# First layer of a two-layer hybrid encoder: attention heads placed between projection units, output projection by weight rows, one-pass gate sums, the norm taken bank by bank

## The chip, the cores and the metric

The kernel runs on one core of a Trainium2 chip. The metric is the device time of one launch in microseconds (us). The changed kernel is compared with the kernel before on the same inputs.

## The reference

One sequence of 256 tokens, width 1024, passes two layers. Each layer has a mixer and a channel mixer, each with an RMS norm ahead of it and a residual addition behind it.

```python
# layer 0, mixer A
h = rmsnorm(x, mix_norm_g[0]); m = rmsnorm(mem, mem_norm_g[0])
mk, mv = split(m @ w_mem_kv[0])                       # 4 heads of 64, 256 memory tokens
q, k, v, fl, qm = split(h @ w_in_a[0])                # 12 FoX heads of 64; fl: 12 gate columns
cum = cumsum(log_sigmoid(fl + b_forget))              # along the sequence
s = (q @ k.T) * 64**-0.5 + cum[query] - cum[key]      # causal, in blocks of 128 queries
y_self = softmax(s) @ v
y_mem = softmax((qm @ mk.T) * 64**-0.5) @ mv
x = x + concat(y_self, y_mem) @ w_out[0]
x = x + swiglu(rmsnorm(x, ffn_norm_g[0]))             # dense, inner width 2816
# shared K and V are projected from x; layer 1: differential attention (6 heads) beside
# memory attention, then 8 experts of inner width 3584, top 2 of 8; a final norm
```

## The kernel before, in words

Weights arrive in units of 128 x 2048 f32 (1 MB) through a ring of 6 `raw` slots that SP fills. ScalarE (ACT) casts a unit to `whi` (L521), VectorE (DVE) subtracts to get `wlo` (L809); both are rings of 3 slots. The activations are split in the same way into `op_hi` and `op_lo`. A product of two f32 matrices is then three one-pass matmuls in the rounded type, hi·hi, hi·lo and lo·hi (`product`, L1359 to L1361). A projection unit p of `PROJ` is 256 weight columns: 8 blocks of the contraction, 3 passes and 2 halves, 48 matmuls of 256 columns (`project`). It fills one PSUM bank, and DVE moves it out (`take(p)`, L851).

Each engine executes its own list in order, and semaphores bind the lists. TensorE's list for layer 0 is:

- `norm_transposes(0)` and unit 0, `norm_transposes(1)` and unit 1: mk and mv from the memory tokens.
- Units 2 to 11: q0 to q2, k0 to k2, v0 to v2, qm. Between them stand the transposes of norm 2 (the memory norm of layer 1), the gate columns (`small_product`), their transposes and the cumulated sums (L1520, L1521).
- `attention_pe(0)`: 12 FoX heads, then 4 memory heads. Scores run up to 4 heads ahead of the values. The score of a FoX head (L1430, L1435, L1438) has, for each of the two query tiles, an f32 matmul of q and k over 64 rows (128 or 256 keys), an f32 matmul over 12 rows that adds -cum[key] (`ident[0:12, h]` by `ncum`), and a bf16 one that adds the causal mask. Three 128x128 transposes of the probabilities (L1456; four for a memory head) and the values (L1483, L1485, L1488) follow. Between them DVE takes maxima (L985, L986) and scales the probabilities (L1026 to L1029); ACT takes exponentials (L605, L607) and copies transposed probabilities (L634).
- Units 12 to 15: the output projection, each 256 columns of `w_out` over all 8 blocks, added to X by `take`. Unit 16 (mk of layer 1), the transposes of norm 3 (`norm_transposes(3)`), unit 17, and then the dense channel mixer.

In the lists of ACT and DVE the splits of coming units stand between these steps. DVE does `angles` (rotary angles, a chain of small operations, L925 to L949) beside late q/k/v units, while nobody waits for them until layer 1.

A norm is: squares with row sums on ACT (L538 or L529), mean and epsilon on DVE (L821), the square root on ACT (L541), reciprocal (L824) and scaling by row and gain (L837, 4 pieces of 128x512) on DVE, then 16 transposes on TensorE (L1372), `op_hi` on ACT (L550) and `op_lo` on DVE (L846). For norm 4, behind the channel mixer of layer 0, DVE waits for the last matmul of the last down-projection unit, adds four banks to X (L1108), ACT squares them, and one mean and one root serve both token tiles:

```python
            split_lo(U_KV + 1)
            dve.wait_ge(unit_used, U_KV)
            # four additions bank -> X, then
            norm_dve(4, X, 5, parts=2)
            norm_fill_lo(4)
```

## Time and profile before

| | |
|---|---|
| Time, three runs | 1620.61, 1621.83 (median), 1622.0 us |
| Span of the profiled execution, from first to last instruction | 1619.5 us (2.3 us under the median) |
| TensorE matmuls busy | 1542.1 us, 95% |
| DVE, ACT busy | 73%, 59% |
| TensorE's share of the chain that ended last | 94% |
| Mean granted TensorE clock | 0.944 of full speed |

"Granted clock" is the share of TensorE's full 2.4 GHz that the chip let through; it has two levels here, 1.00 and 0.50. The busy time of matmuls is modelled and overlapping, so the distance from one start to the next says more than a duration. A row "x2" for one f32 matmul means that it is recorded as two. A stretch "A:B" is in microseconds from the start of the span.

### The profile page before, as it was taken

The page shows a single profiled execution, that of the slowest core. Times are in us where ns is not written, and L with a number is a line of the kernel's source. Part 1 is how long each engine was busy: PE and PEld are TensorE (multiplying, and loading weights), DVE is VectorE, ACT ScalarE, POOL GpSimd, SP SyncE. Part 2 cuts the span into 40 slices and gives each one's busy share as a digit, 9 for nine tenths or more (in the row PEclk, how much of TensorE's full clock was granted, in tenths as well). Part 3 has the DMA queues.
Part 4 walks back from the last instruction along what each step waited for, and adds up shares of the span by engine and source line. Part 5 has one row for each costly group of instructions (what it writes and reads, how often), then busy time and mean ns, then how long its engine had stood idle before and what let it go on. Part 6 is the DMA issues. An engine that isn't in the chain of part 4 may idle for free.

```text
span 1619.5 us, 21334 instructions
## 1 busy us (share of the span) xinstructions
PE 1542.1 (95%) x8083; PEld 1291.0 (80%) x8083; DVE 1181.3 (73%) x1013; ACT 954.4 (59%) x885; POOL 14.4 (1%) x44
## 2 busy tenths in 40 slices
PE   4999999999899879999999999999999999999996
PEld 4975598999796668887887887887888888888884
DVE  4642254445675657988989889888888988888885
ACT  4432344343433537777776767767776776776774
POOL 2000000000000000000000000000000000000000
PEclk8985599999897879999999999999999999999998
DMA  9640044645542237999999998998998998998991
GB/s 301 199 156 0 1 144 156 208 156 201 185 145 94 110 138 271 380 338 334 372 357 332 372 378 307 372 376 312 370 374 311 370 374 311 369 383 284 324 352 76
DMA packets 210235, 428.93 MB, mean 265 GB/s; under 512 B 6800, under 2 KB 62096, under 8 KB 210176
## 3 DMA queue, kind: packets, MB, share of 16 engines
q1 hardware_dynamic: 208880, 424.18, 73.4%
q0 software_dynamic: 1296, 3.96, 1.0%
q8 instruction: 38, 0.62, 0.2%
q14 instruction: 21, 0.17, 0.0%
HBM read 427.06 MB, written 1.05 MB: 264 GB/s over the span
## 4 chain that ended last, share of the span: by engine, by line
PE 94%; DVE 3%; DMA 1%; ACT 1%; issue 1%; DVEq 0%; SPq 0%; ACTq 0%
PE bank L1359 27%; PE bank L1361 27%; PE bank L1360 27%; PE bank L1430 3%; PE bank L1634 2%; PE bank L1709 2%; PE bank L1635 1%; PE bank L1435 1%; DMA raw<-in_w_mem_kv_dram 1%; PE bank L1483 1%; PE bank L1456 1%; PE bank L1372 1%; PE bank L1438 1%; PE bank L1425 1%; DVE wlo L809 0%
## 5 line engine op out<-in xcount | busy, mean ns | idle before, releaser
L809 DVE TENSOR_TENSOR wlo<-raw,whi 128x2048 fp32r<-128x2048 f32 x397 | 907.4, 2290 | 216.4 <-ACT whi L521 215.3
L521 ACT CAST whi<-raw 128x2048 fp32r<-128x2048 f32 x397 | 758.1, 1914 | 276.7 <-PE bank L1361 263.6
L1359 PE MATMUL bank<-whi,op_hi 128*128 128x512 f32 (+1 forms) x1248 | 456.7, 366 | 5.4 <-DVE op_lo L1169 1.7
L1361 PE MATMUL bank<-whi,op_lo 128*128 128x512 f32 (+1 forms) x1248 | 450.6, 361 | 0.0
L1360 PE MATMUL bank<-wlo,op_hi 128*128 128x512 f32 (+1 forms) x1248 | 450.3, 361 | 0.0
L1359 PEld LDWEIGHTS bank<-whi,op_hi 128*128 128x128 f32 x1248 | 237.2, 190 | 44.1 <-DVE wlo L809 3.4
L1361 PEld LDWEIGHTS bank<-whi,op_lo 128*128 128x128 f32 x1248 | 237.1, 190 | 36.1
L1360 PEld LDWEIGHTS bank<-wlo,op_hi 128*128 128x128 f32 x1248 | 237.4, 190 | 33.7
L1359 PE MATMUL bank<-whi,h2T_hi 128*128 128x512 f32 x536 | 210.8, 393 | 0.0
L1361 PE MATMUL bank<-whi,h2T_lo 128*128 128x512 f32 x536 | 208.9, 390 | 0.0
L1360 PE MATMUL bank<-wlo,h2T_hi 128*128 128x512 f32 x536 | 208.7, 389 | 0.0
L1359 PE MATMUL bank<-op_hi,whi 128*128 128x256 f32 x512 | 146.1, 285 | 16.7 <-DVE op_lo L846 13.7
L1360 PE MATMUL bank<-op_lo,whi 128*128 128x256 f32 x512 | 145.5, 284 | 0.0
L1361 PE MATMUL bank<-op_hi,wlo 128*128 128x256 f32 x512 | 145.5, 284 | 0.0
L1361 PEld LDWEIGHTS bank<-whi,h2T_lo 128*128 128x128 f32 x536 | 100.6, 188 | 21.4
L1360 PEld LDWEIGHTS bank<-wlo,h2T_hi 128*128 128x128 f32 x536 | 100.8, 188 | 20.0
L1359 PEld LDWEIGHTS bank<-whi,h2T_hi 128*128 128x128 f32 x536 | 100.7, 188 | 19.9
L1359 PEld LDWEIGHTS bank<-op_hi,whi 128*128 128x128 f32 x512 | 99.0, 193 | 17.7 <-DVE op_lo L846 14.1
L1360 PEld LDWEIGHTS bank<-op_lo,whi 128*128 128x128 f32 x512 | 99.0, 193 | 0.4
L1361 PEld LDWEIGHTS bank<-op_hi,wlo 128*128 128x128 f32 x512 | 98.9, 193 | 0.0
L738 ACT CAST h2T_hi<-bank 128x512 fp32r<-128x512 f32 x56 | 32.9, 588 | 66.3 <-PE bank L1709 66.3
L985 DVE TENSOR_REDUCE negm<-bank 128x1 f32<-128x128 f32 (+1 forms) x32 | 10.3, 323 | 66.3 <-PE bank L1438 58.2
(247 smaller groups left out, 1034.8 us busy)
## 6 DMA issues: line engine op xcount, KB each, us to landing
raw<-in_w_gate_up_moe_dram SPq DMA_DIRECT2D x223, 1024.0 KB, 6.8
raw<-in_w_down_moe_dram SPq DMA_DIRECT2D x109, 1024.0 KB, 6.9
raw<-in_w_gate_up_dense_dram SPq DMA_DIRECT2D x22, 1024.0 KB, 5.1
raw<-in_w_down_dense_dram SPq DMA_DIRECT2D x11, 1024.0 KB, 5.0
raw<-in_w_in_a_dram SPq DMA_DIRECT2D x10, 1024.0 KB, 11.6
raw<-in_w_out_dram SPq DMA_DIRECT2D x8, 1024.0 KB, 5.1
raw<-in_w_kv_shared_dram SPq DMA_DIRECT2D x6, 1024.0 KB, 5.1
raw<-in_w_mem_kv_dram SPq DMA_DIRECT2D x4, 1024.0 KB, 11.8
```

Source lines behind the costliest of these rows:

```text
L521: a.copy(whi[:, c % SPLIT, :], src).then_inc(hi_ready, 1)
L738: a.copy(h2T_hi[j % 2][:], bank[tb_bank(f"T{j}")][:]).then_inc(h2_hi, 1)
L809: d.tensor_tensor(wlo[:, c % SPLIT, :], src, whi[:, c % SPLIT, :].bitcast(F32), ALU.subtract).then_inc(lo_ready, 1)
L1359: m.matmul(dst, sh, mh, start=start and i == 0, stop=False)
L1360: m.matmul(dst, sh, ml, start=False, stop=False)
L1361: last = m.matmul(dst, sl, mh, start=False, stop=stop and i == n - 1)
L1372: last = m.transpose(bank[g][:, P * c:P * (c + 1)], hn[:, t, P * k:P * (k + 1)], ident[:])
L1425: mm = m.matmul(b[:, MEM * t:MEM * (t + 1)], qmT[po:po + HD, c, sl], mkT[layer][po:po + HD, c, :], start=True, stop=True)
L1430: m.matmul(b[:, o0:o0 + w], qT[po:po + HD, c, sl], kT[po:po + HD, c, 0:w], start=True, stop=False)
L1435: m.matmul(b[:, o0:o0 + w], ident[0:FOX_H, h:h + 1].to_broadcast([FOX_H, P]), ncum[:, 0:w], start=False, stop=False)
L1634: m.matmul(dst, st_hi, mv_hi, start=start, stop=False)
L1709: last = m.transpose(bank[tb_bank(f"T{j}")][:, P * c:P * (c + 1)], h2[j % 2][:, P * c:P * (c + 1)], ident[:])
```

## The change

- The heads of layer 0 are handled one by one in `HEADS0`, 4 memory heads first and then 12 FoX heads, and TensorE's list becomes a loop of 17 steps. Step s issues the dense work of `DENSE0[s]` (a whole unit or one half of it, 12 units in all), then transposes of head s, values of head s-1, and scores of head s+2. The lists of ACT and DVE are loops over the same steps.
- Unit order: mk, mv, qm, then q, k, v for four heads at a time.
- Output projection by weight rows (`out_rows`): a unit is 256 rows of `w_out`, all 1024 columns, summed over the four units in banks 4 to 7. It is 24 matmuls of 512 columns. The last unit stays behind the loop, after `norm_transposes(2)`, which moves there from the second unit.
- The term -cum[key] is stored as a rounded part in rows 0 to 11 and the remainder in rows 32 to 43 of `ncum`, zero elsewhere, and enters by one pass over 128 rows with a 0/1 column of `pick`, in place of the f32 matmul.
- DVE and ACT do the rotary angles before the attention; `take(1)`, the split of unit 4 and `take(P_QM)` follow them on DVE.
- Norms 3 and 4 are taken bank by bank: each bank of the last product raises a semaphore, and the first token tile is normalised ahead of the second (`sum_norm`). The split of unit U_KV+1 now stands behind the norm on DVE. Other norms have mean, root and reciprocal for each tile apart.
- The gain of norm 2 shares the tile of the first gain and is loaded by GpSimd after norm 0 has been applied.

```diff
-PROJ = ([("mk", 0), ("mv", 0)]
-        + [("q", i) for i in range(3)] + [("k", i) for i in range(3)] + [("v", i) for i in range(3)] + [("qm", 0)]
-        + [("out", i) for i in range(4)] + [("mk", 1), ("mv", 1)]
+PROJ = ([("mk", 0), ("mv", 0), ("qm", 0)]
+        + [(what, i) for i in range(3) for what in "qkv"]
+        + [("rows", i) for i in (3, 0, 1, 2)] + [("mk", 1), ("mv", 1)]
...
+HEADS0 = [("mem", h) for h in range(MEM_H)] + [("fox", h) for h in range(FOX_H)]
+N0 = len(HEADS0)
+DENSE0 = [[(3, 0), (3, 1)], [(4, 0), (4, 1)], [(5, 0), (5, 1)], [(6, 0), (6, 1)], [(7, 0), (7, 1)], [(8, 0)], [(8, 1)],
+          [(9, 0), (9, 1)], [(10, 0)], [(10, 1)], [(11, 0)], [(11, 1)], [(12, 0)], [(12, 1)], [(13, 0), (13, 1)],
+          [(14, 0)], [(14, 1)]]
+def ended_in(s):
+    return [p for p, c in DENSE0[s] if c == 1]
+def takes(p):
+    return sum(what != "rows" for what, _ in PROJ[:p + 1])
...
+def proj_bank(p):
+    if p < P_OUT0:
+        return 4 + p % 3
+    return 4 + (p - P_M1 if p < P_KV else p % 4)
...
+        pick = sb("pick", [P, FOX_H], F32R)
         negm = sb("negm", [P, 32, NT])
...
+            pool.dma_start(start_gain[2], mem_norm_g[1:2, :].to_broadcast([P, D])).then_inc(start_gain_in[2], 16)
             for n in range(3, 8):
                 load_gain(n)
...
-            split_until(4)
+            norm_squares(2, tok, mem_in)
+            for t in range(NT):
+                norm_sqrt(2, t)
             act.wait_ge(small_in, 16 * 9)
             a.copy(small_hi[:], small_w[:]).then_inc(small_hi_ready, 1)
+            split_until(4)
+            act.wait_ge(ang_ready, 1)
+            a.activation(sinv[:], ang[:, 1], ACT.Sin)
+            a.activation(cosv[:], ang[:, 2], ACT.Sin).then_inc(sin_ready, 1)
...
+                if s >= 3:
+                    act.wait_ge(pT_ready, s - 2)
+                pr, b = prob[s % 3], bank[s % 2]
+                a.activation(pr[:, 0:w0], b[:, 0:w0], ACT.Exp, bias=negm[:, s, 0:1], accum_out=rsum[:, s, 0:1])
+                a.activation(pr[:, w0:w0 + w1], b[:, w0:w0 + w1], ACT.Exp, bias=negm[:, s, 1:2],
+                             accum_out=rsum[:, s, 1:2]).then_inc(exp_done, 1)
...
+            exp0(0)
+            exp0(1)
+            split_until(6)
...
+            for s in range(N0 + 1):
+                for u in ended_in(s):
+                    split_until(u + 4)
+                if s < N0:
+                    copy0(s)
+                if s and s % 2 == 0:
+                    pair_hi0(s // 2 - 1)
+                if s + 2 < N0:
+                    exp0(s + 2)
+            norm_fill_hi(2)
+            sqrt_table()
+            sum_norm(3, x_out, 0)
...
+            def sum_norm(n, banks, ready, counts, done):
+                for q in range(4):
+                    if q == 3:
+                        norm_mean(n, 0, 2)
+                    t, cols = q // 2, slice(512 * (q % 2), 512 * (q % 2 + 1))
+                    dve.wait_ge(ready[q], counts[q])
+                    d.tensor_tensor(X[:, t, cols], X[:, t, cols], bank[banks + q][:], ALU.add).then_inc(done, 1)
+                norm_scale(n, 0)
+                apply_gain(n, X, n, 0, 0)
+                norm_mean(n, 1, 2)
+                apply_gain(n, X, n, 0, 1)
+                norm_scale(n, 1)
+                for h in range(2):
+                    apply_gain(n, X, n, 1, h)
...
+            dve.wait_ge(ident_ready, 1)
+            d.tensor_tensor(pick[:], ident[:, 0:FOX_H], ident[:, 32:32 + FOX_H], ALU.add).then_inc(pick_ready, 1)
+            angles_start()
+            angles(1)
+            angles(2)
+            take(1)
+            split_until(5)
+            lambda_dots()
+            take(P_QM)
+            dve.wait_ge(flT_ready, 1)
+            d.tensor_copy(small_T, bank[7][0:FOX_H, 0:SEQ]).then_inc(flT_out, 1)
...
+                cum = bank[7][0:FOX_H, SEQ:2 * SEQ]
+                step(d.tensor_scalar(ncum[0:FOX_H, :], cum, -1.0, None, ALU.mult))
+                d.scalar_tensor_tensor(out=ncum[32:32 + FOX_H, :], in0=cum, scalar=-1.0,
+                                       in1=ncum[0:FOX_H, :].bitcast(F32), op0=ALU.mult,
+                                       op1=ALU.subtract).then_inc(ncum_ready, 1)
...
+            max0(0)
+            max0(1)
+            forget_sums()
+            split_until(6)
+            normalise0(0)
+            for s in range(N0 + 1):
+                for u in ended_in(s):
+                    if PROJ[u][0] != "rows":
+                        take(u)
+                if s == 0:
...
+                if s == 1:
+                    decay_rows()
+                if s + 2 < N0:
+                    max0(s + 2)
+                if s + 1 < N0:
+                    normalise0(s + 1)
+                if s and s % 2 == 0:
+                    pair_lo0(s // 2 - 1)
+                for u in ended_in(s):
+                    split_until(u + 4)
+            norm_fill_lo(2)
+            sum_norm(3, 4, [acc_ready] * 3 + [unit_used], [1, 2, 3, P_M1], x_out)
...
             split_lo(U_KV)
+            sum_norm(4, 0, [acc_ready] * 3 + [unit_used], [4, 5, 6, U_KV], x_added)
             split_lo(U_KV + 1)
-            dve.wait_ge(unit_used, U_KV)
-            for t in range(NT):
-                for h in range(2):
-                    cols = slice(512 * h, 512 * (h + 1))
-                    d.tensor_tensor(X[:, t, cols], X[:, t, cols], bank[2 * t + h][:], ALU.add).then_inc(x_added, 1)
-            dve.wait_ge(x_added, 4)
-            norm_dve(4, X, 5, parts=2)
...
+            def out_rows(p, parts=(0, 1)):
+                _, i = PROJ[p]
+                first, final = p == P_OUT0, p == P_M1 - 1
+                hi, lo = op_hi[Y_BUF[0]], op_lo[Y_BUF[0]]
+                if 0 in parts:
+                    pe.wait_ge(lo_ready, p + 1)
+                    pe.wait_ge(fill_lo, int(FILL[1]) + 2 * (p - P_OUT0) + 2)
+                    if first:
...
+                for t in parts:
+                    sl = slice(P * t, P * (t + 1))
+                    for h in range(2):
+                        cols = slice(512 * h, 512 * (h + 1))
+                        last = product(bank[4 + 2 * t + h][:],
+                                       [((hi[:, 2 * i + k, sl], lo[:, 2 * i + k, sl]), (wh[:, k, cols], wl[:, k, cols]))
+                                        for k in range(2)], start=first, stop=final)
+                        if final and not (t == 1 and h == 1):
+                            last.then_inc(acc_ready, 1)
+                if 1 in parts:
+                    last.then_inc(unit_used, 1)
...
+            def score0(s):
+                kind, h = HEADS0[s]
+                if s >= 2:
+                    pe.wait_ge(exp_done, s - 1)
+                if s == 0:
+                    pe.wait_ge(proj_out, takes(P_QM))
+                if kind == "fox" and h == 0:
+                    pe.wait_ge(ncum_ready, 1)
+                    pe.wait_ge(pick_ready, 1)
+                if kind == "fox" and h % 4 == 0:
+                    pe.wait_ge(proj_out, takes(P_A + 3 * (h // 4) + 1))
...
+                    w, o0 = P * (t + 1), P * t
+                    m.matmul(b[:, o0:o0 + w], qT[po:po + HD, c, sl], kT[po:po + HD, c, 0:w], start=True, stop=False)
+                    m.matmul(b[:, o0:o0 + w], pick[:, h:h + 1].to_broadcast([P, P]), ncum[:, 0:w], start=False,
+                             stop=False)
+                    mm = m.matmul(b[:, o0 + w - P:o0 + w], ident_bf[:], causal[:], start=False, stop=True)
...
+                pe.wait_ge(pT_out, s + 1)
+                if kind == "fox" and h % 4 == 0:
+                    pe.wait_ge(proj_out, takes(P_A + 3 * (h // 4) + 2))
+                if s % 2 == 0 and pr:
+                    pe.wait_ge(fill_lo, int(FILL[1]) + pr)
...
-            for p in range(P_A, P_OUT0):
-                project(p)
-                if p == P_A:
...
-                    pe.wait_ge(logf_ready, 1)
-                    pe.wait_ge(consts, 1)
-                    m.matmul(bank[3][0:FOX_H, 256:512], fg[:, 2, 0, :], upper[:], start=True, stop=False)
-                    m.matmul(bank[3][0:FOX_H, 384:512], fg[:, 2, 1, :], upper[:, 0:P], start=False,
-                             stop=True).then_inc(cum_ready, 1)
-            pe.wait_ge(ncum_ready, 1)
-            pe.wait_ge(proj_out, P_OUT0)
-            attention_pe(0)
-            for p in range(P_OUT0, P_M1 + 1):
-                project(p)
+            project(P_QM)
+            pe.wait_ge(small_lo_ready, 1)
+            pe.wait_ge(small_hi_ready, 1)
+            small_product(bank[7], 1, 0, FOX_H).then_inc(flT_ready, 1)
+            score0(0)
+            score0(1)
+            pe.wait_ge(flT_out, 1)
+            small_transposes(bank[7], FOX_H).then_inc(fl_ready, 1)
+            for s in range(N0 + 1):
+                for p, c in DENSE0[s]:
+                    if PROJ[p][0] == "rows":
+                        out_rows(p, (c,))
+                    else:
+                        project(p, (c,))
+                if s == 1:
+                    forget_cum()
+                if s < N0:
+                    transposes0(s)
+                if s:
+                    values0(s - 1)
+                if s + 2 < N0:
+                    score0(s + 2)
+            norm_transposes(2)
+            out_rows(P_M1 - 1)
+            project(P_M1)
             norm_transposes(3)
             project(P_M1 + 1)
```

## Rows read from the trace of the kernel before

**Rows 1.** The page's costliest groups of instructions: busy us, mean ns, idle before.

```profile
L809 DVE TENSOR_TENSOR wlo<-raw,whi 128x2048 fp32r<-128x2048 f32 x397 | 907.4, 2290 | 216.4 <-ACT whi L521 215.3
L521 ACT CAST whi<-raw 128x2048 fp32r<-128x2048 f32 x397 | 758.1, 1914 | 276.7 <-PE bank L1361 263.6
```

**Rows 2.** Busy time by stretch: us, PE, PEld, DVE, ACT, POOL, clock, DMA, GB/s.

```profile
106.90:199.65 92.75, 90.45 (x253) 48.96 (x253) 26.28 (x89) 28.00 (x91) 0.00 (x0) 0.54 0.06 20
109.50:121.50 12.00, 12.00 (x29) 6.23 (x29) 2.90 (x7) 2.85 (x13) 0.00 (x0) 0.50 0.26 87
```

**Rows 3.** Timeline, TensorE, first FoX scores: start, us, instruction.

```profile
106.90 0.46 PE L1430 MATMUL bank<-attn 64*128 64x128 f32 x2 [1.18 <-DVE attn L868]
107.29 0.48 PE L1435 MATMUL bank<-ncum,ident 12*128 12x128 f32 x2
107.70 0.23 PE L1438 MATMUL bank<-causal,ident_bf 128*128 128x128 bf16 x1
...
108.49 0.69 PE L1435 MATMUL bank<-ncum,ident 12*128 12x256 f32 x2
109.11 0.23 PE L1438 MATMUL bank<-causal,ident_bf 128*128 128x128 bf16 x1
109.27 0.79 PE L1430 MATMUL bank<-attn 64*128 64x128 f32 x2
```

**Rows 4.** Timeline, TensorE, one FoX head in the middle of the attention.

```profile
155.49 0.79 PE L1430 MATMUL bank<-attn 64*128 64x128 f32 x2
...
159.53 0.85 PE L1456 MATMUL bank<-ident,prob 128*128 128x128 f32 x3
160.31 1.11 PE L1483 MATMUL bank<-probT,attn 128*64 128x256 f32 x2
...
161.78 0.79 PE L1430 MATMUL bank<-attn 64*128 64x128 f32 x2
```

**Rows 5.** Timeline, TensorE, memory heads of layer 0, then one of layer 1.

```profile
194.72 0.66 PE L1456 MATMUL bank<-ident,prob 128*128 128x128 f32 x4
195.31 0.65 PE L1483 MATMUL bank<-probT,mv 128*64 128x256 f32 x2
...
196.32 0.65 PE L1456 MATMUL bank<-ident,prob 128*128 128x128 f32 x4
...
540.43 1.14 PE L1425 MATMUL bank<-attn 64*128 64x256 f32 x8
```

**Rows 6.** Timeline, TensorE, behind unit 2: transposes, unit 3, gate columns.

```profile
47.87 1.91 PE L1372 MATMUL bank<-ident,hn 128*128 128x128 f32 x16
49.54 0.36 PE L1359 MATMUL bank<-op_hi,whi 128*128 128x256 f32 x1
...
55.36 0.28 PE L1359 MATMUL bank<-op_hi,small_hi 128*12 128x256 f32 x1
```

**Rows 7.** Timeline, DVE, scaling of norm 2.

```profile
40.06 2.74 DVE L837 SCALAR_TENSOR_TENSOR hn<-tok,stat,attn 128x512 f32<-128x512 f32 x4
```

**Rows 8.** Busy time by stretch: from the first to the last operation of `angles`.

```profile
98.44:99.85 1.41, 1.41 (x14) 1.41 (x13) 1.21 (x8) 0.00 (x0) 0.00 (x0) 1.00 0.10 22
104.53:106.16 1.63, 1.19 (x10) 0.98 (x9) 1.39 (x10) 0.00 (x0) 0.00 (x0) 1.00 0.16 38
```

**Rows 9.** Busy time by stretch: norm 4, and memory attention of layer 1.

```profile
426.50:430.00 3.50, 0.00 (x0) 0.00 (x0) 2.54 (x6) 2.56 (x8) 0.00 (x0) 1.00 0.84 283
430.50:440.00 9.50, 7.25 (x33) 6.88 (x34) 7.92 (x10) 4.15 (x5) 0.53 (x1) 0.50 0.18 57
542.00:555.00 13.00, 8.70 (x50) 5.58 (x50) 9.50 (x33) 9.49 (x30) 0.00 (x0) 1.00 0.00 0
```

**Rows 10.** Timeline, DVE and TensorE, norm 4.

```profile
426.23 2.48 DVE L1108 TENSOR_TENSOR X<-X,bank 128x512 f32<-128x512 f32 x4 [1.15 <-PE bank L1361]
...
430.45 2.74 DVE L837 SCALAR_TENSOR_TENSOR hn<-X,stat,gain 128x512 f32<-128x512 f32 x4
...
436.39 0.58 PE L1359 MATMUL bank<-whi,op_hi 128*128 128x256 f32 x1 [1.40 <-DVE op_lo L846]
```

More of the change, by code:

```diff
@@ L331, in proj_source @@
             if what == "out":
-                return out_v[p >= P_OUT1][:, :, c:c + WIDE]
+                return out_v[1][:, :, c:c + WIDE]
+            if what == "rows":
+                return out_v[0][:, 2 * i:2 * i + 2, :]
             if what == "kd":
@@ L625, in fill @@
                     act.wait_ge(pv_ready, rb0 + r + 1)
-                    a.copy(op_hi[Y_BUF[layer]][:, c, :], bank[5 + (r // 2) % 2][:, 0:SEQ]).then_inc(fill_hi, 1)
+                    a.copy(op_hi[Y_BUF[1]][:, c, :], bank[5 + (r // 2) % 2][:, 0:SEQ]).then_inc(fill_hi, 1)
                 exps(AHEAD - 1)
@@ L702, in _ @@
             out_squares(P_OUT1, [U_KV + 13, U_MOE, U_MOE + 1])
-            norm_act(6, None, None)
+            for t in range(NT):
+                norm_sqrt(6, t)
             norm_fill_hi(6)
@@ L974, in attention_dve @@
-            def attention_dve(layer):
-                scores, outs, last = attention_plan(layer)
-                sb0, rb0 = S_BASE[layer], R_BASE[layer]
+            dve.wait_ge(ident_ready, 1)
[8 more added lines that the diff above has]
+            dve.wait_ge(flT_ready, 1)
@@ L977, in attention_dve @@
+            norm_fill_lo(2)
+            sum_norm(3, 4, [acc_ready] * 3 + [unit_used], [1, 2, 3, P_M1], x_out)
+            split_lo(U_FFN)
+            take(P_M1)
+            norm_fill_lo(3)
+            split_lo(U_FFN + 1)
+            take(P_M1 + 1)
+            def attention_dve():
+                scores, outs, last = attention_plan()
+                sb0, rb0 = S1, R1
                 done = [0]
@@ L1408, in small_transposes @@
                 return last
-            def attention_pe(layer):
-                scores, outs, last_s = attention_plan(layer)
-                sb0, rb0 = S_BASE[layer], R_BASE[layer]
+            def score0(s):
+                kind, h = HEADS0[s]
+                if s >= 2:
+                    pe.wait_ge(exp_done, s - 1)
[6 more added lines that the diff above has]
+                    pe.wait_ge(proj_out, takes(P_A + 3 * (h // 4) + 1))
+                b = bank[s % 2]
+                po, c = HD * (h % 2), h // 2
+                for t in range(NT):
+                    sl = slice(P * t, P * (t + 1))
+                    if kind == "mem":
+                        mm = m.matmul(b[:, MEM * t:MEM * (t + 1)], qmT[po:po + HD, c, sl], mkT[0][po:po + HD, c, :],
+                                      start=True, stop=True)
+                        continue
+                    w, o0 = P * (t + 1), P * t
[3 more added lines that the diff above has]
+                    mm = m.matmul(b[:, o0 + w - P:o0 + w], ident_bf[:], causal[:], start=False, stop=True)
+                mm.then_inc(score_ready, 1)
@@ L1498, in attention_pe, with forget_cum @@
                 values(len(outs) - 1)
+            def forget_cum():
+                pe.wait_ge(logf_ready, 1)
+                pe.wait_ge(consts, 1)
+                b = bank[7]
+                m.matmul(b[0:FOX_H, SEQ:2 * SEQ], fg[:, 2, 0, :], upper[:], start=True, stop=False)
+                m.matmul(b[0:FOX_H, SEQ + P:2 * SEQ], fg[:, 2, 1, :], upper[:, 0:P], start=False,
+                         stop=True).then_inc(cum_ready, 1)
             pe.wait_ge(ident_ready, 1)
@@ L1560, in ffn_down @@
                                         for k, s in enumerate(sls)], start=first, stop=final)
+                        if final and not (t == 1 and h == 1):
+                            last.then_inc(acc_ready, 1)
                 last.then_inc(unit_used, 1)
```

389 lines of the change are left out of this document (210 added, 179 removed).

## The prediction

> **What bounds the kernel now.** I read the page's shares first: TensorE is busy 95% of the span and has 94% of the chain that ended last, so the time is TensorE's list, its idle gaps and its clock. The costliest groups say that the splits of weights, the largest work of DVE and ACT, cost 2.29 and 1.91 us a unit [rows 1]; a projection unit costs TensorE 5.8 us [rows 6], so in the projections both engines have room. Then I read busy time by stretch. The attention of layer 0 lasts 92.75 us, with TensorE busy 90.45 of them at a mean clock of 0.54, DVE and ACT busy 26 and 28, and almost no transfer; inside it stands a stretch of 12 us, busy throughout, at 0.50 [rows 2]. The reader is to see a stage in which the bounding engine never rests and yet runs at 1.2 GHz.
>
> **Prices at either clock.** The first FoX score is still at the full clock: 106.90 to 109.27, 2.37 us, of which the two gate matmuls take 0.41 and 0.62 [rows 3]. In the middle a head takes 6.29 us at half clock: score 4.04, three transposes 0.78, values 1.47 [rows 4]. The score is the only part seen at both, a factor of 1.70. A memory head at the full clock has 0.59 for transposes and 1.01 for values, and its score 1.14 [rows 5].
>
> **The change part by part.** The sum is made against the span of 1619.5 us; the median of the runs shown is 2.3 us more, and I add the difference at the end.
>
> *Dense work.* Units 2 to 17 stay sixteen units of 5.8 us [rows 6]; the row-wise output units have half as many matmuls of twice the columns, the same stream. The transposes of norms 2 and 3 (1.67 us each [rows 6]), the gate columns and the cumulated sums only move. Zero, if the clock stays full in them.
>
> *Gate sums.* Two f32 matmuls of 1.03 us together [rows 3] become two one-pass matmuls over the same columns. The nearest row is the projection, 5.82 us for 48 passes of 256 columns, 0.12 each [rows 6]. I take 0.23 for both. The bounds are no gain (a stationary operand with stride 0 is in no row for this type) and all of 1.03, 0 to 12.4 us over 12 heads; I take the value nearest to the projection's row. The split of ncum adds one DVE operation, once.
>
> *Heads at the full clock.* This is the main term. FoX: score 2.37 - 1.03 + 0.23 = 1.57, transposes three quarters of 0.59 = 0.44, values 1.47 by 1.70 = 0.86; 2.87 us, 34.4 for twelve. Memory: 1.14 + 0.59 + 1.01 = 2.74, 11.0 for four. Together 45.4 us, where 92.75 and the 1.18 of idle ahead of them [rows 2, 3] stood: 93.9.
>
> Whether the clock stays full is read from where it fell. It was 1.00 on the first FoX score and 0.50 from 109.5 on [rows 2, 3], and 1.00 through 3.5 us of idle behind the channel mixer, then 0.50 [rows 9]. In the memory attention of layer 1 it stayed 1.00 for 13 us though TensorE was busy only 8.70 of them, with no projection at all [rows 9]. So short gaps do not lower it; a stretch of nothing but FoX scores and heads did. In the new loop a head's 2.87 us stand between pieces of 2.9 or 5.8 us of projection. I take full clock throughout the loop.
>
> The Trainium skill, page "TensorE: Matmul & The Clock Gate", section "Why this matters for your kernels", asks for no idle gaps of TensorE above about 3 us between bursts of matmuls. By this rule alone a list that is never idle should not lose its clock, and the main term of this sum would be nothing; the 12 busy microseconds at 0.50 contradict it [rows 2], and the measurement decides. For a real idle gap, as in norm 4 [rows 9], the trace agrees.
>
> *A new wait ahead of the loop.* `score0(0)` needs `take(P_QM)`. On DVE, behind the scaling of norm 2, which ends at 42.8 [rows 7], there stand in order: small_lo (0.3, estimate), the split of unit 3 (2.3), pick and the start of the angles (0.8, estimate), two passes of angles (1.41 and 1.63 [rows 8]), `take(1)` (0.6). That is 49.8. (Small terms without a row, here and below, are estimates on the scale of rows 7 and 8: 0.69 for a piece of 128x512, 0.2 for an operation on a few columns, and down from there.) ACT may cast unit 4 only after the two sines, which wait for the angles: 49.5 + 0.4 + 1.9 = 51.8. Then DVE has the split 2.3, the lambda sums 0.7 and `take(P_QM)` 0.7: 55.5. TensorE has finished unit 2 at 47.87 [rows 6] and the gate columns 2.8 later, at 50.7, and waits 4.8 us. Queued behind the waiting instruction is everything of the loop. Bounds: 3 us if the small operations overlap, 6.5 if the waits between them add up. The gap costs clock too: as in norm 4 I expect the fall, two memory scores at half (2.28 by 1.70, 1.6 more), and the first dense piece at half for about as long as behind norm 4, where the product resumed at 436.39 and the clock was still 0.50 up to 440.0 [rows 9, 10]: near 4 us at half speed, 2.0 lost. Together 8.4; bounds 3 and 12.
>
> *Other waits in the loop.* Probabilities of head s+1 are needed behind the dense piece of step s+1. DVE begins its maxima when that piece begins and needs 0.7 for them and 0.85 for the scaling, less than the shortest piece of 2.9 [rows 6]. The split behind it ends about 4.8 + 2.3 us past the end of unit u and is needed two units later. ACT needs 1.9 for the cast, then 0.5, 0.4 and 1.1. A take of 0.7 stands ahead of the maxima only where a unit ended, and lies beside 2.9 us of transposes, values and score. So zero; bounds 0 and 1 us a step. At the loop's end `norm_transposes(2)` waits with its fourth bank for the last pair, whose copy stands on ACT behind a cast: values 0.9, transposes 1.3, against 1.95 + 0.4 + 0.5 and a signal: 0.8 us of idle. The norm of layer 0's output then lies beside unit 16, as before.
>
> *Norm 4.* Before, the chain from the first addition to the product ran from 426.23 to 436.39 [rows 10]. Now three additions and three squares lie beside the last product. From 426.2: last addition 0.7, square 0.85, first reciprocal and piece beside it; mean and roots 0.7 net, remaining pieces to 430.5. Then the split of unit U_KV+1, 2.3, which used to lie beside the product and now stands ahead of the low halves; these take 2.5. Product at 435.4, a gain of 1.0. Without that split it would be 3. Bounds 0 and 3 (the latter with the clock kept). Norms 0 to 2 and 6 get a few operations of 0.17 more; where they lie on the path (norm 6) the first tile starts earlier: zero, bounds ±0.5.
>
> *The start.* One gain load of 0.5 MB goes behind norm 0 on GpSimd's queue. It competes with the first weights a little later and not less. Zero, bounds ±1.5. It is needed near 40 us and has over 20 us.
>
> **The sum.** 93.9 - 45.4 - 8.4 - 0.8 + 1.0 = 40.3 us. The span becomes 1579.2 and the median 1581.5 us.
>
> **The rivals.**
>
> *The clock falls in some steps.* Ten of the 17 steps hold only half a unit, so there 2.87 us of head stand by 2.9 us of dense work. For it: the fall on FoX scores with TensorE busy [rows 2, 3]. Against it: 13 us of thin memory attention at 1.00 [rows 9]. A step at half costs 5.8 by 0.70, 4.0 us. With half of the ten steps it is 20 us: 1602; with all ten 1622.
>
> *Hand-offs cost.* The signals of three engines cross in every step, and one late link (a take ahead of the maxima, a cast ahead of the copy) stops TensorE. At 0.7 us in 17 steps it is 12 us: 1593. Against it are the margins above, more than 1.3 us at each link.
>
> *Slower.* The mixture holds TensorE at half clock for the whole loop, so the dense work, full before, pays as well. Place: steps 0 to 16; price: 69 us of dense and 43 of heads by 0.70, 78 us, less the 40 gained: 1660. It decides from the point where the clock is at half for more than half of the loop. For it speaks only that the attention never recovered by itself in 85 us; against it that 4 us of projection brought it back each time.
>
> *The one pass is not what it says.* Where the one-pass gate matmul costs as much as the old pair, the heads come to 55 us: 1591.
>
> **Chances.** Forecast 0.72; some steps at half 0.10; hand-offs 0.08; one pass without gain 0.05; slower 0.05. The range reaches from 1572 (short wait, clock kept in norm 4, small products cheap) to 1602. About 0.2% is what a measurement of this kernel can tell from no change, 3.2 us; only the slower rival and the worst end of the clock's case are there. Faster 0.93, same 0.02, slower 0.05.
>
> **What would show it.** In the stretches of the changed profile, 60 to 175 us has a clock of 1.00 and TensorE busy over 95%. The gate line has two one-pass matmuls a head with starts 0.1 to 0.13 us before the next. One idle gap of 3 to 6.5 us stands ahead of the first memory score, released by DVE, and the clock is 0.50 behind it. Unit 17 ends near 197 us. The product behind norm 4 resumes about 9.3 us after the last matmul of the channel mixer. From there on every distance is as before. The forecast is wrong if clock rows of 0.50 recur past 65 us, if idle time ahead of the transposes or values adds up to more than 5 us, or if the later stages change by more than 2 us.

## The result and the profile after

The changed kernel takes **1577.42 us** (median of 4 runs, 1575.57 to 1578.95), beside 1621.22 us for the kernel before in the same session: a ratio of 0.9735, 95% interval [0.9722, 0.9748], 43.8 us less. The profiled execution of the changed kernel spans 1573.8 us, where the one before spanned 1619.5. Two executions of the kernels below, one of dense_first (2386.29 us) and one of turns_of_2 (2170.47 us), ran at mean granted clocks of 0.59 and 0.645 in place of some 0.95, and no ratio below uses them.

First the shares and the chain on the page after, then the two groups that answer to [rows 1].

```profile
PE 1495.9 (95%) x7963; PEld 1264.8 (80%) x7963; DVE 1181.2 (75%) x1030; ACT 953.9 (61%) x883; POOL 15.6 (1%) x45
...
PE 92%; DVE 4%; ACT 2%; DMA 1%; issue 1%; DVEq 0%; SPq 0%; ACTq 0%
...
L897 DVE TENSOR_TENSOR wlo<-raw,whi 128x2048 fp32r<-128x2048 f32 x397 | 907.4, 2290 | 202.2 <-ACT whi L556 201.2
L556 ACT CAST whi<-raw 128x2048 fp32r<-128x2048 f32 x397 | 758.1, 1914 | 271.3 <-PE bank L1516 257.7
```

TensorE still bounds the kernel at the same 95%, and DVE and ACT do the same work on weights in the same time. What went is TensorE's own time: 46.2 us less busy. Where, is seen in the busy time by stretch of the kernel after (columns as in [rows 2]): the wait ahead of the first score, the piece behind it, the whole loop, and the pieces behind the two later gaps.

```profile
50.15:53.93 3.78, 0.01 (x2) 0.00 (x1) 3.57 (x6) 1.63 (x3) 0.00 (x0) 1.00 0.09 18
53.93:57.50 3.57, 3.57 (x16) 2.74 (x17) 1.83 (x7) 0.78 (x3) 0.00 (x0) 0.52 0.94 291
57.50:170.90 113.40, 112.60 (x724) 92.08 (x723) 55.75 (x112) 49.53 (x102) 0.34 (x1) 1.00 0.34 109
206.86:211.10 4.24, 4.24 (x23) 4.24 (x24) 2.75 (x2) 0.20 (x1) 0.00 (x0) 0.60 0.72 225
392.50:395.50 3.00, 2.97 (x14) 2.97 (x15) 3.00 (x3) 0.00 (x0) 0.00 (x0) 0.52 0.74 258
```

The reader is to see the third row beside the first of [rows 2]: 0.54 has become 1.00, for 113 us. ("Dense" work is that of the projection units, matmuls of all 128 rows one behind the other.) All the idle time in those 113 us is one wait of 0.80. The timeline of TensorE shows it, and one head in the middle of the loop, between one dense piece, whose last matmul starts at 104.29, and the next, which starts at 107.26. It answers to [rows 3, 4, 6].

```profile
53.93 1.98 PE L1614 MATMUL bank<-mkT,attn 64*128 64x256 f32 x8 [3.77 <-DVE attn L988]
...
63.55 0.66 PE L1632 MATMUL bank<-ident,prob 128*128 128x128 f32 x4 [0.80 <-DVE prob L1100]
64.14 1.13 PE L1614 MATMUL bank<-mkT,attn 64*128 64x256 f32 x4
...
104.41 0.49 PE L1632 MATMUL bank<-ident,prob 128*128 128x128 f32 x3
104.83 0.65 PE L1648 MATMUL bank<-probT,attn 128*64 128x256 f32 x2
105.32 0.38 PE L1650 MATMUL bank<-probT,attn 128*64 128x128 f32 x2
105.63 0.48 PE L1618 MATMUL bank<-attn 64*128 64x128 f32 x2
106.04 0.33 PE L1619 MATMUL bank<-ncum,pick 128*128 128x128 f32 x1
106.21 0.23 PE L1621 MATMUL bank<-causal,ident_bf 128*128 128x128 bf16 x1
106.37 0.70 PE L1618 MATMUL bank<-attn 64*128 64x256 f32 x2
107.00 0.38 PE L1619 MATMUL bank<-ncum,pick 128*128 128x256 f32 x1
107.22 0.23 PE L1621 MATMUL bank<-causal,ident_bf 128*128 128x128 bf16 x1
107.26 0.36 PE L1514 MATMUL bank<-whi,op_hi 128*128 128x256 f32 x1
...
172.98 0.66 PE L1529 MATMUL bank<-ident,hn 128*128 128x128 f32 x4 [0.52 <-DVE op_lo L1107]
```

A FoX head takes 2.85 us in place of 6.29 [rows 4]: transposes 0.42, values 0.80, score 1.63. The two gate matmuls take 0.17 and 0.22 by the distance to the next start.

**One ruler for all kernels.** TensorE's first product starts at 27.19 us before and 26.52 after, and between 23.96 and 27.72 in the twelve kernels below, whose starts hardly differ. So I measure from that product on:

| from the first product, us | channel mixer resumes (unit G1) | product behind norm 4 | end of span |
|---|---|---|---|
| before | 223.51 | 409.20 | 1592.31 |
| after | 180.34 | 366.01 | 1547.28 |
| before_one_pass | 209.16 | 396.15 | 1577.20 |
| dense_first | 225.06 | 410.76 | 1596.27 |
| f32_gate | 188.01 | 373.69 | 1556.53 |
| turns_of_2 | 197.61 | 383.30 | 1566.53 |
| turns_of_2_norm_first | 183.23 | 367.42 | 1552.71 |
| turns_of_4 | 230.47 | 414.66 | 1599.05 |
| turns_of_4_norm_first | 222.77 | 408.45 | 1594.27 |
| angles_late | 177.19 | 362.87 | 1548.44 |
| norm4_once | 180.22 | 369.27 | 1552.74 |
| score_pairs | 172.52 | 358.22 | 1540.76 |
| mixer_start_and_split_late | (no gap) | 359.14 | 1543.24 |
| all_together | (no gap) | 345.01 | 1516.28 |

By the start of the channel mixer 43.17 of the 45.03 us between the two kernels are there. Each row is one execution, the profiled one. From the product behind norm 4 to the end, where all kernels but all_together have the same list on TensorE, the rows lie between 1181.05 and 1185.82 us, so the last column can't show gains of 1 to 4 us; the first one is what the accounts below use.

### The profile page after: what moved, and what is told of

Same layout as the page of the kernel before. It is cut to its first block, busy times and chain, and to the rows that moved or that the text cites. A ratio compares the mean times of both kernels' runs of the same rounds, so it can differ in the third digit from the quotient of the medians.

```text
span 1573.8 us, 21113 instructions
## 1 busy us (share of the span) xinstructions
PE 1495.9 (95%) x7963; PEld 1264.8 (80%) x7963; DVE 1181.2 (75%) x1030; ACT 953.9 (61%) x883; POOL 15.6 (1%) x45
## 4 chain that ended last, share of the span: by engine, by line
PE 92%; DVE 4%; ACT 2%; DMA 1%; issue 1%; DVEq 0%; SPq 0%; ACTq 0%
PE bank L1514 28%; PE bank L1516 27%; PE bank L1515 27%; PE bank L1881 2%; PE bank L1956 2%; PE bank L1882 1%; PE bank L1677 1%; DMA raw<-in_w_mem_kv_dram 1%; DVE wlo L897 1%; PE bank L1618 1%; PE bank L1648 1%; PE bank L1529 1%; ACT whi L556 0%; DVE X L1410 0%; PE bank L1619 0%
## 5 line engine op out<-in xcount | busy, mean ns | idle before, releaser
L1514 PE MATMUL bank<-whi,op_hi 128*128 128x512 f32 (+1 forms) x1216 | 451.9, 372 | 7.1 <-DVE op_lo L966 3.9
L1516 PE MATMUL bank<-whi,op_lo 128*128 128x512 f32 (+1 forms) x1216 | 445.0, 366 | 0.0
L1515 PE MATMUL bank<-wlo,op_hi 128*128 128x512 f32 (+1 forms) x1216 | 444.5, 366 | 0.0
L1514 PEld LDWEIGHTS bank<-whi,op_hi 128*128 128x128 f32 x1216 | 230.8, 190 | 46.7 <-DVE op_lo L966 4.2
L1516 PEld LDWEIGHTS bank<-whi,op_lo 128*128 128x128 f32 x1216 | 230.5, 190 | 37.5
L1515 PEld LDWEIGHTS bank<-wlo,op_hi 128*128 128x128 f32 x1216 | 231.0, 190 | 34.9
L756 ACT ACTIVATE prob<-bank 128x512 f32<-128x512 f32 x11 | 6.6, 597 | 86.1 <-PE bank L1516 86.1
```

The costliest lines, as they stand in the source:

```text
L1514: m.matmul(dst, sh, mh, start=start and i == 0, stop=False)
L1515: m.matmul(dst, sh, ml, start=False, stop=False)
L1516: last = m.matmul(dst, sl, mh, start=False, stop=stop and i == n - 1)
```

## The experiments

My theory was that dense work between the heads keeps TensorE's clock at 1.00, and that the one-pass gate saves a little beside it. The rivals were that the 12-row gate matmuls had lowered the clock, and that only hand-offs are hidden.

### The one-pass gate, with and without the turns

f32_gate, against the changed kernel:

```
-        ncum = sb("ncum", [P, SEQ], F32R)
+        ncum = sb("ncum", [P, SEQ])
-   m.matmul(..., pick[:, h:h + 1].to_broadcast([P, P]), ncum[:, 0:w], ...
+   m.matmul(..., ident[0:FOX_H, h:h + 1].to_broadcast([FOX_H, P]), ncum[0:FOX_H, 0:w], ...
```

> The changed kernel with one part undone: the sums of the forget gate come again from a 12-row f32 matmul (ident rows, ncum f32) instead of the one-pass 128-row one. Theory (the one pass saves only what the loop shows at the full clock: before 1.03 us a head, now 0.39): 12 heads x 0.64 = 7.7 us more than the changed kernel's 1577.4, so 1585. Rival A (the gate was hidden, or the price of 0.23 us a head that was predicted is the true one): 1577 or 1587. Rival B (matmuls of 12 rows inside a step also let the clock fall): the loop's granted clock is below 1.00 and the time is 1595 or more.

Measured: 1587.08 us, ratio to before 0.9793 [0.9775, 0.9811]; clock 1.00 throughout the loop; 7.67 us more at the mixer's start, where the theory said 7.7. The medians differ by 9.7 us, and 1587 was also the price by the rival in which a gate pair costs 0.23 us; what refutes that rival are the distances in the timeline after, 0.17 and 0.22, together 0.39. Matmuls of 12 rows do not lower the clock in this loop.

before_one_pass is the same edit the other way round, on the kernel before, with the zeroed rows and the pick columns.

> The kernel before, with the one-pass gate sums alone (128-row F32R operand, zeroed rows, the pick columns); heads still stand back to back behind the projections. Theory (the clock is at 0.50 there whatever the gate's form; a gate costs twice 1.03 us before and twice 0.39 us after): 12 x 1.28 = 15.4 us less than 1621.2: 1606. Rival A (what lowered the clock were the matmuls of 12 rows): the granted clock is 1.00 in the attention and the time is 1576 to 1585. Rival B (the gates lay beside a wait for VectorE): under 5 us less, 1616 or more.

Measured: 1605.89 us, 0.9913 [0.9899, 0.9927], 14.35 us less at the mixer's start. The clock is still at half: busy time by stretch, then one head of it.

```profile
110.00:180.00 70.00, 68.63 (x196) 39.96 (x196) 23.71 (x86) 22.82 (x85) 0.00 (x0) 0.51 0.05 15
```

```profile
150.30 0.79 PE L1439 MATMUL bank<-attn 64*128 64x128 f32 x2
151.03 0.47 PE L1444 MATMUL bank<-ncum,pick 128*128 128x128 f32 x1
151.30 0.33 PE L1447 MATMUL bank<-causal,ident_bf 128*128 128x128 bf16 x1
151.56 1.22 PE L1439 MATMUL bank<-attn 64*128 64x256 f32 x2
152.71 0.58 PE L1444 MATMUL bank<-ncum,pick 128*128 128x256 f32 x1
...
155.47 0.79 PE L1439 MATMUL bank<-attn 64*128 64x128 f32 x2
```

A head takes 5.17 us, 1.12 less than in [rows 4]. The first rival is out: with the 12-row gate matmuls gone the clock still falls. Together with f32_gate this gives the price of the one pass in both surroundings: 14.35 us at half clock and 7.67 at the full one, 1.2 and 0.64 a head.

### The turns

dense_first takes the turns away: all q, k and v units in step 0.

```
+DENSE0: step 0 = units 3 to 11; steps 12 to 16 as before (rows)
+   (step 0)  take(u); split_until(u + 4)     # unit by unit
```

> The changed kernel with all nine q, k and v units ahead of the heads' step 0 and nothing dense in steps 1 to 11; the units by weight rows stay where they are. Theory (dense work between the heads is what holds TensorE's clock): the granted clock is 0.50 through the 11 steps, a FoX head takes 5.0 to 5.8 us in place of 2.9, so 23 to 32 us more than 1577.4: 1600 to 1609. Rival (the gain is only that hand-offs are hidden by dense work, or the one-pass gate alone holds the clock): the granted clock stays at 1.00 and what comes is idle time between heads, 0 to 12 us: 1577 to 1589.

Measured: 1625.82 us, 1.0032 [1.002, 1.0045], 0.3% more than the kernel before the change, and above what the theory gave. The clock is at 0.50 from 110.3 to 189, but for 3.5 us; what I had not priced is in the waits. The fall itself came inside a wait of 2.97 us, for the sums of the gates (`forget_cum`), which the missing dense work had covered as well. Timeline of TensorE, two heads of it:

```profile
138.75 0.33 PE L1621 MATMUL bank<-causal,ident_bf 128*128 128x128 bf16 x1
140.46 0.90 PE L1632 MATMUL bank<-ident,prob 128*128 128x128 f32 x3 [1.37 <-DVE prob L1098]
...
147.25 0.90 PE L1632 MATMUL bank<-ident,prob 128*128 128x128 f32 x3 [1.37 <-DVE prob L1098]
```

From the second head on, each waits 1.37 us or a little more for its probabilities, 14.3 us in 11 waits with the 0.32 of the first. In step s DVE takes the maxima of head s+2 before it scales head s+1. The score of head s+2 is the last thing on TensorE in step s, and the transposes of head s+1 are the next, unless dense work stands between. So a hand-off of 1.37 us is built into the new order, and only the dense piece covers it. Compared with before_one_pass (same gates, heads together) dense_first is 15.90 us later at the mixer's start; its waits of 14.3 and 2.97 us are more than that. The whole change, by that point, is then the sum of three measured steps: one pass -14.35, everything else but the turns (new head loop, unit order, output by rows, angles early) +15.90, turns -44.72; together -43.17. The last step holds two things that dense_first doesn't part, the waits that dense work covers and the clock.

turns_of_2 has whole units only from step 5 on, so that two heads stand together.

```
+DENSE0: step 5 = unit 8, 6 none, 7 = 9, 8 = 10, 9 none, 10 = 11, 11 none, 12 = rows, 13 none, ...
```

> The changed kernel with whole units only, from step 5 on: two heads stand back to back (5.8 us of head work at the full clock) and then a whole unit (11.5 us alternately with them). Theory A (a stretch of heads of 6 us between dense units is still held): granted clock 1.00 throughout, 1577 (within 1.5). Theory B (the halves were needed: the clock falls in each of the stretches of two heads): five stretches, each 1.5 to 3 us longer, 1585 to 1592, and 0.50 shows in the windows of these heads.

Measured: 1594.66 us, 0.9842 [0.9826, 0.9859]; at the mixer's start 17.27 us more than the changed kernel, above theory B. Timeline of TensorE and the stretch behind it:

```profile
109.09 0.23 PE L1619 MATMUL bank<-causal,ident_bf 128*128 128x128 bf16 x1
110.70 0.55 PE L1630 MATMUL bank<-ident,prob 128*128 128x128 f32 x3 [1.37 <-DVE prob L1098]
...
114.88 0.56 PE L1512 MATMUL bank<-op_hi,whi 128*128 128x256 f32 x1
115.24 0.41 PE L1513 MATMUL bank<-op_lo,whi 128*128 128x256 f32 x1
```

```profile
110.70:118.80 8.10, 8.10 (x33) 6.49 (x34) 3.72 (x7) 2.00 (x8) 0.00 (x0) 0.58 0.39 131
```

The 1.37 us appear between the two heads and the clock falls within 1.3 us (the starts from 112.0 on are at half speed), for the second head and 3.9 us of the unit behind it. The same wait stands in four places, 5.5 us together, and behind each of the four the clock falls. So either two heads or the wait lowers the clock; the next kernel separates them by turning round the two calls on DVE, which shortens the wait and moves no work of TensorE:

```
-   max0(s + 2); normalise0(s + 1)
+   normalise0(s + 1); max0(s + 2)
```

> turns_of_2 with VectorE's order in a step turned round: it normalises head s+1 before it takes the maxima of head s+2. In turns_of_2 the second head of each pair waited 1.37 us for its probabilities, because the maxima ahead of them wait for the score that TensorE issues last in the step. Theory A (the idle 1.37 us is what lets the clock fall): the waits go, the granted clock is 1.00 and the time is that of the changed kernel, 1577 to 1579. Theory B (two heads in a row let the clock fall by themselves): only the idle time goes, 5.5 of the 17.3 us, and 0.50 still shows: 1588 to 1590.

Measured: 1579.27 us, 0.9754 [0.9737, 0.9771], beside the changed kernel's 0.9735 within the intervals. Theory A holds: same heads in a row, no 1.37 us wait, clock 1.00. At the mixer's start it is 2.89 us behind the changed kernel. The stretch with two heads:

```profile
106.00:110.00 4.00, 4.00 (x23) 2.45 (x21) 2.42 (x7) 2.73 (x5) 0.00 (x0) 1.00 0.46 160
110.00:112.00 2.00, 2.00 (x12) 1.44 (x13) 1.97 (x3) 1.10 (x5) 0.00 (x0) 1.00 0.00 0
```

Two calls changed places and 14.4 us went at the mixer's start, of which about 3 was idle time and the rest half clock behind it. Three waits of 0.80 and one of 1.30 (ahead of the last head's values; turns_of_2 has it too) remain in the loop, and the clock stays at 1.00 from 60 to 180 us. So the added wait is what the clock needed to fall here, but its length alone is no rule: 1.30 did nothing, and layer 1, below, passes waits of 1.92 at 1.00.

turns_of_4 has three units, then four heads; turns_of_4_norm_first the same with DVE's order turned round.

```
+DENSE0: step 0 = units 3, 4, 5; step 4 = 6, 7, 8; step 8 = 9, 10, 11; step 12 = two row units; 16 = one
```

> The changed kernel with three units and then four heads back to back, four times (11.7 us of head work at the full clock between dense stretches of 16.5 us). Theory A (a stretch this long loses the clock): 0.50 shows in the later part of each of the stretches, each 4 to 9 us longer, four of them: 1593 to 1613. Theory B (the mean load over a longer time decides, and it is that of the changed kernel): clock 1.00, 1577 to 1583, the rest idle time between heads.

> turns_of_4 with VectorE's order turned round in the same way. Theory A (the idle time lets the clock fall): most of the 1.37 us waits go and the clock holds, 1577 to 1590. Theory B (head work in a row lets it fall): 11 waits, some 15 us, go, and the clock stays at 0.50 in the later part of each stretch: 1607 to 1615.

Measured: 1629.42 us, 1.0061 [1.0041, 1.0081], and 1618.16 us, 0.9996 [0.9984, 1.0009]. Both miss upward, because of waits that I had not foreseen: with three units ending at once, DVE has three splits ahead of the next probabilities (119.80 to 126.48 in the second kernel, for the wait that ends at 127.20). What is left of them with DVE's order turned round, waits of TensorE (total, times, longest) and a stretch:

```profile
PE bank L1630 <- DVE prob L1098: 15.1, 4, 5.2
```

```profile
122.00:124.00 2.00, 0.61 (x4) 0.28 (x2) 2.00 (x2) 0.00 (x0) 0.00 (x0) 0.85 0.40 49
124.00:126.00 2.00, 0.00 (x0) 0.00 (x0) 2.00 (x2) 0.00 (x0) 0.00 (x0) 0.50 0.99 401
...
134.00:136.00 2.00, 2.00 (x7) 1.05 (x6) 0.71 (x3) 0.60 (x3) 0.00 (x0) 0.50 0.05 8
```

The clock falls in a wait of 4.58 us and the heads behind it do not bring it back. Whether four heads without any wait would keep it, this pair does not tell.

### The reorderings

angles_late moves the angles and their sines into steps 5 to 8, and the small lambda products behind the first maxima:

```
-   angles_start(); angles(1); angles(2)      # ahead of take(1)
+   (s == 5) angles_start(); angles(1)   (s == 6) angles(2)   ACT: Sin at s == 8
```

> The changed kernel with the rotary angles (VectorE) and their sines (ScalarE) moved from ahead of the first score into steps 5 to 8 of the loop, and the lambda products behind the first maxima. Theory (the wait of 3.8 us ahead of the first score, and the 3.3 us at half clock behind it, come from these instructions): the wait goes, the clock stays at 1.00, 3.8 + 1.7 = 5.5 us less than 1577.4: 1572. Rival (the next hand-off is as late: the first head's probabilities, now 0.8 us late, or the unit's weights): at most 2 us less, 1575 to 1577, with idle time ahead of the first transposes.

Measured: 1574.56 us, 0.9712 [0.9696, 0.9728]. The first score starts without a wait, but the next link is late. Timeline:

```profile
47.96 1.14 PE L1617 MATMUL bank<-mkT,attn 64*128 64x256 f32 x8
...
56.75 0.66 PE L1635 MATMUL bank<-ident,prob 128*128 128x128 f32 x4 [1.49 <-DVE prob L1097]
```

A split that waits for ACT stands ahead of the first scaling, and behind these 1.49 us the clock is again at half for 3.5 us. 3.15 us are won at the mixer's start, between the theory's 5.5 and the rival's 2. By the end of the span they are gone in this execution (1548.44 beside 1547.28): with the same list the clock stayed at half longer behind three later gaps (1.4 us behind norm 4, 1.1 in layer 1's attention, 1.5 in the router).

norm4_once makes norm 4 wait for all four banks:

```
-   sum_norm(4, 0, [acc_ready] * 3 + [unit_used], [4, 5, 6, U_KV], x_added)
+   sum_norm(4, 0, [unit_used] * 4, [U_KV] * 4, x_added)
```

> The changed kernel with norm 4 waiting for the whole of the channel mixer's last product before any of the four banks is added (the bank-by-bank part undone for this norm). Theory (the overlap is worth the first adds and squares that now lie beside the last product): the gap between the last product and the next grows from 8.85 to 10.3 us or somewhat more, 1579 to 1580.5. Rival (the overlap is worth nothing since the last bank decides): within 0.5 of 1577.4.

Measured: 1578.75 us, 0.9742 [0.9728, 0.9756], whose interval overlaps that of the changed kernel. The profile tells more: from the last matmul of the mixer to the product behind norm 4, start to start, it is 11.42 us, 9.08 after. The overlap is worth 2.34.

mixer_start_and_split_late reorders DVE in two places:

```
+   split_lo(G1)      # ahead of ffn_mul(0), first turn of the loop written out
-   split_lo(U_KV + 1); norm_fill_lo(4)
+   norm_fill_lo(4); split_lo(U_KV + 1)
```

> The changed kernel with two reorderings on VectorE that are read each from its own stage. (1) The split of the channel mixer's second gate unit ahead of its first product: theory, the 3.0 us of idle time goes and with it 1.5 us of half clock, 4.5 less from the loop's end to the mixer's end; rival, the unit behind it is as late, 1 us less at most. (2) The split of the second key and value unit behind norm 4's last step: theory, 2.3 us less from the mixer's end to the product behind norm 4 (now 8.85); rival, an idle gap ahead of the second unit gives them back. Together 1577.4 - 6.8 = 1570.6.

Measured: 1569.28 us, 0.969 [0.9675, 0.9706]. The mixer has no gap and keeps 1.00; its last matmul is 4.66 us earlier (4.5 expected), and from there to the product behind norm 4 it is 6.87 in place of 9.08 us, 2.21 less (2.3). No gap stands ahead of the second unit. Both rivals are out.

score_pairs issues two heads' scores together, at even steps:

```
+   for t in range(NT):
+       QK(s, t); QK(s + 1, t)               # partitions 0-63, then 64-127
+       gate(s, t); mask(s, t); gate(s + 1, t); mask(s + 1, t)
```

> The changed kernel with the scores of two heads issued together at every second step: the 64-row products of the head on partitions 0 to 63 and of the one on 64 to 127 stand next to each other. Theory (two such products run side by side, as the memory heads' pairs at 1.14 us for two against 1.07 us for one show): per pair of FoX heads some 0.9 us less, six pairs, and 1.0 for the second pair of memory heads: 6.5 us less, 1571. Rival A (they run one behind the other): 1577. Rival B (two heads' worth of head work in a row brings the clock down or a hand-off late): 1580 or more.

Measured: 1571.35 us, 0.9698 [0.9685, 0.9712], 7.82 us less at the mixer's start. Timeline; x4 is two heads:

```profile
108.16 0.49 PE L1619 MATMUL bank<-attn 64*128 64x128 f32 x4
108.58 0.33 PE L1623 MATMUL bank<-ncum,pick 128*128 128x128 f32 x1
...
109.10 0.70 PE L1619 MATMUL bank<-attn 64*128 64x256 f32 x4
109.73 0.38 PE L1623 MATMUL bank<-ncum,pick 128*128 128x256 f32 x1
```

0.42 and 0.63 us for two heads, what one head took after.

all_together joins angles_late, score_pairs and the two reorderings; besides, DVE scales before it takes maxima, the first scaling stands ahead of its split, and layer 1's scores go in pairs.

> The changed kernel with angles_late, score_pairs, mixer_start and split_late, and besides: VectorE normalises before it takes maxima, the first head's probabilities come ahead of the split of the third unit of the loop, and the second layer's scores are issued in pairs too. Theory (each gain is at a stage of its own): angles and first probabilities 5, score pairs 7.8, mixer and split 6.8, second layer's pairs 6 x 0.9 = 5.4 where its heads are not waiting: 25 us less than 1577.4: 1552. Rival (half clock behind the other gaps takes some back, as in angles_late, and layer 2 waits for VectorE): 1558 to 1562.

Measured: **1545.74 us, 0.9545 [0.9525, 0.9565]**, better than the theory. In layer 1 it takes 109.3 us from norm 4 to the output projection in place of 119.3. What went there is not waits, for TensorE's idle time rose from 9.3 to 15.7 us, but half clock: after, TensorE was at 0.50 from 460 to 494; here it is 1.00 among waits of 1.92 us ahead of 454.99 and 459.62, and at 0.50 for some 7 us behind them. One stretch of the kernel after, then two of all_together:

```profile
467.00:470.00 3.00, 3.00 (x10) 1.71 (x8) 1.50 (x5) 0.48 (x1) 0.00 (x0) 0.50 0.00 0
...
452.00:455.00 3.00, 1.08 (x10) 0.47 (x9) 1.85 (x7) 1.34 (x7) 0.00 (x0) 1.00 0.00 0
458.00:461.00 3.00, 1.38 (x11) 1.26 (x13) 2.85 (x10) 1.07 (x7) 0.00 (x0) 1.00 0.00 0
```

Which of the changes to layer 1 keeps the clock there, no run separates. Busy time by stretch in all_together, from ahead of the first score to the loop's end:

```profile
48.00:159.00 111.00, 111.00 (x779) 92.94 (x777) 62.50 (x141) 54.25 (x110) 0.34 (x1) 1.00 0.39 132
```

Not a gap, and the full clock all the way.

## Why the prediction was right, point by point

Forecast 1581.5, measured 1577.4; the saving was 40.3 by the sum and 45.7 in the profiled spans.

- *Heads at the full clock* (45.4 for sixteen): right. A FoX head was put at 2.87 and takes 2.85; score 1.57 became 1.63, transposes 0.44 and values 0.86 became 0.42 and 0.80.
- *Gate sums* (0.23 a head): mis-sized, 0.39: the pair was priced by columns alone, and at 128 columns the matmul is not half of that at 256 (0.17, 0.22). Worth 12 x 0.16 = 1.9 us; the smaller parts above make up for it. The rival "no gain" is refuted by f32_gate.
- *Why the clock stays* was the weak step. I wrote that "short gaps do not lower it; a stretch of nothing but FoX scores and heads did". In the new loop it is the other way round: two heads in a row kept the clock, and with a wait of 1.37 us between them they lost it, four times of four. In the kernel before, a wait of 1.18 us stands right ahead of the fall [rows 3]; whether it was needed there, or the heads behind it lose the clock by themselves, no run shows. In the attention of layer 1 before, a wait of 0.88 us ends at 501.21, the clock falls at 505.2 and stays at 0.50 to 539. My evidence, 13 us at 1.00 [rows 9], begins three microseconds behind that stretch.
- The Trainium skill, page "TensorE: Matmul & The Clock Gate", section "Why this matters for your kernels", puts the harmful gap at about 3 us; in this loop 1.37 us among heads was enough, and the measurement decides. The gap of 2.98 us ahead of unit G1, among dense units, comes with half clock in nine of the twelve kernels that have it and not in before, turns_of_2_norm_first and turns_of_4.
- *That the attention never recovered by itself* was misread. In the kernel before, the clock is back at 1.00 at 194.6, among the memory heads [rows 5] and 5 us ahead of the next product; in dense_first it is back among heads from 130.7 to 134.2. What holds is that heads can stay at half for long (0.51 over 70 us in before_one_pass), where in turns_of_2 the clock was back after 3.9 us of dense work.
- *A new wait ahead of the loop* (8.4): right in place and kind, too large. The wait was 3.77 for 4.8; the two memory scores took 1.91 at half for the 3.9 I had, because two adjacent 64-row scores run side by side (the x8 of [rows 5] is two heads, and I had read it as one); half clock ended at 57.5. With the 0.80 us wait for the first probabilities, which I had put at zero, it comes to about 6 (3.77 + 1.7 of half clock + 0.80).
- *Other waits in the loop* (zero): right but for the 0.80, no other idle time to 170.9. The margin I worked out, maxima and scaling against the shortest dense piece, is the one that dense_first removes. Loop's end: 0.8 forecast, 0.52 measured.
- *Norm 4* (1.0): from the last matmul to the product it was 10.58 us between starts before and is 9.08, so 1.5 less; both parts of the term, the overlap and the split that stands in the way, show at 2.34 and 2.21.
- *The start* (zero): 0.67 in the profile, inside what executions differ by.
- *Later stages* (unchanged): the mixer's first gap of 3.0 us, which had left the clock alone before, now brings half clock for some 3.4 us. That costs the 1.5 us which norm 4 gives: from unit G1 to the product behind norm 4 it is 185.69 us before and 185.67 after. Against it the clock was at half for a shorter time behind norm 4 and in the router. These are of the size of the difference between the profiled saving, 45.7, and that of the medians, 43.8.
- *The rivals.* "The clock falls in some steps" and "hand-offs cost" turned out to be one mechanism, which the dense pieces cover: a wait of 1.37 in the open brings both (turns_of_2, 1594.7 us). That this lies close to the 1593 and 1602 that I gave them is luck, for I had priced other waits and other falls. The slower rival (mixture at half clock) did not appear in any kernel with short turns.

## What to carry to other kernels

When TensorE is busy and yet at half clock, look for a short wait at the head of the stretch, remove it and look again; until then it is a guess. Price a wait among thin matmuls (heads: 64 or 128 rows, 128 or 256 columns) at its own length and at several microseconds of half clock behind it: here two calls in the other order were worth 14 us, of which 3 were idle. Alternating with dense work pays twice, for it covers the hand-off and the clock stays or soon comes back, but it also hides an order that is bad by itself; turn that round before changing how the turns are dealt. Products over 64 rows should stand in adjacent pairs, one on partitions 0 to 63 and one on 64 to 127.

## What was not expected of the hardware

- Two 64-row f32 matmuls, one on partitions 0 to 63 and one on 64 to 127, run side by side when adjacent: from start to next start two memory heads' scores take 1.07 us (angles_late, x8 at 47.96, next at 49.03) and one head's takes 1.06 (after, x4 at 64.14, next at 65.20). It was worth 7.8 us in score_pairs.
- How long the clock stays at half behind the same gap, and whether it falls at all, varies between executions: from the router's product to its dispatch it is 7.67 us after, 9.19 before, 9.72 in turns_of_4, for the same work. Gains of 1 to 2 us in one place can be lost in the next, as in angles_late.
- The granted clock of the record can be wrong. In the profile after, the first three microseconds of the first product read 1.00, with starts 0.21 us apart; in f32_gate the same matmuls read 0.50, and at a real 1.00 they stand 0.12 apart, so check a clock against the distances between starts. The line of the kernel after:

```profile
26.52:29.52 3.00, 3.00 (x14) 3.00 (x15) 2.72 (x7) 2.19 (x3) 0.00 (x0) 1.00 1.10 351
```
